# A gated delta rule on ready 32x32 block inverses: seven units of matmuls a step in place of ten, the inverses made in five batches, and the step's loads cut into pieces

## The reference, cut to what matters

```
def gated_delta_chunked(q, k, v, g, beta):          # chunks of 64
    gcum = cumsum(g)                                 # within a chunk
    lower = where(strict, (k*beta) @ k.T * decay, 0)
    sol = triangular_solve(lower + I, [v*beta, k*beta*exp(gcum)])
    u, w = sol
    attn = where(causal, q @ k.T * decay, 0)
    # for each chunk, in order, from state = 0:
    v_new = u - w @ state
    o     = (q*exp(g_i)) @ state + attn @ v_new
    state = state*exp(g_last) + (k*exp(g_last-g_i)).T @ v_new
```

## Time and profile before

| | |
|---|---|
| median of 3 runs | 2506.84 us (2503.91 to 2508.79) |
| the profiled execution | 2497.62 us, its span 2495.9 us |
| TensorE busy | 2326.8 us (93%) |
| VectorE busy | 1422.2 us (57%) |
| ScalarE busy | 1059.5 us (42%) |
| GpSimd busy | 409.1 us (16%) |
| granted TensorE clock, mean | 0.971 |

### The profile page before, as it was taken

How to read it: one execution, slowest core, us unless ns; L and a number is a source line. 1 busy time by engine, 2 the same in 40 slices (tenths; PEclk the granted TensorE clock), 3 DMA queues, 4 the chain that set the end, 5 groups by cost and what they waited for, 6 DMA issues and landing times. The chain is left out here.

```text
span 2495.9 us, 48533 instructions
## 1 busy us (share of the span) xinstructions
PE 2326.8 (93%) x20242; PEld 2071.0 (83%) x20242; DVE 1422.2 (57%) x1792; ACT 1059.5 (42%) x1561; POOL 409.1 (16%) x393
## 2 busy tenths in 40 slices
PE   6999999999999999778878999899999999999996
PEld 5777888999999888677854555599999999999996
DVE  6555311245555286343445458777777777777775
ACT  4666310011111186000035553266666666666664
POOL 1000000012111176433323110000010000100001
PEclk8999999999999999898989999999999999999998
DMA  3333422268676476755544431477778777787765
GB/s 121 89 88 106 141 82 105 72 182 280 203 217 203 154 206 196 231 156 155 155 155 143 149 121 64 178 265 264 255 261 279 272 254 272 263 270 261 267 226 200
DMA packets 174025, 471.69 MB, mean 189 GB/s; under 512 B 57216, under 2 KB 102912, under 8 KB 141088
## 3 DMA queue, kind: packets, MB, share of 16 engines
q1 hardware_dynamic: 160800, 423.08, 50.6%
q0 software_dynamic: 13024, 45.70, 6.4%
HBM read 365.15 MB, written 107.49 MB: 189 GB/s over the span
## 5 line engine op out<-in xcount | busy, mean ns | idle before, releaser
L78 DVE TENSOR_TENSOR ex_w_rest<-weights,ex_w_rounded 128x2048 fp32r<-128x2048 f32 x192 | 439.5, 2290 | 203.9 <-ACT ex_w_rounded L2755 202.0
L2755 ACT CAST ex_w_rounded<-weights 128x2048 fp32r<-128x2048 f32 x192 | 365.8, 1906 | 12.7 <-PEq L48 12.7
L2647 PE MATMUL ex_g_acc<-ex_xt,ex_w_rounded 128*128 128x320 f32 x1024 | 270.4, 347 | 2.1 <-ACT ex_xt L2767 2.1
L2647 PE MATMUL ex_u_acc<-ex_xt,ex_w_rounded 128*128 128x320 f32 x1024 | 271.7, 348 | 0.0
L2648 PE MATMUL ex_g_acc<-ex_xt,ex_w_rest 128*128 128x160 f32 x1024 | 242.1, 236 | 0.0
L2648 PE MATMUL ex_u_acc<-ex_xt,ex_w_rest 128*128 128x160 f32 x1024 | 242.1, 236 | 0.0
L2648 PEld LDWEIGHTS ex_g_acc<-ex_xt,ex_w_rest 128*128 128x128 f32 x1024 | 196.5, 192 | 0.0
L2648 PEld LDWEIGHTS ex_u_acc<-ex_xt,ex_w_rest 128*128 128x128 f32 x1024 | 196.4, 192 | 0.0
L2647 PEld LDWEIGHTS ex_g_acc<-ex_xt,ex_w_rounded 128*128 128x128 f32 x1024 | 193.1, 189 | 2.5 <-issue 2.5
L2647 PEld LDWEIGHTS ex_u_acc<-ex_xt,ex_w_rounded 128*128 128x128 f32 x1024 | 193.1, 189 | 0.2
L85 PE MATMUL ch_wide<-normed,ch_w_rounded 128*128 128x512 f32 x384 | 153.7, 400 | 2.9 <-PEq L48 2.2
(11 more groups left out here) (421 smaller groups left out, 5541.1 us busy)
## 6 DMA issues: line engine op xcount, KB each, us to landing
weights<-in_w_expert SPq DMA_DIRECT2D x192, 1024.0 KB, 5.2
laq<-sc_laq SPq DMA_DIRECT2D x20, 1024.0 KB, 4.1
dl_la<-laq SPq DMA_DIRECT2D x20, 1024.0 KB, 6.0
tk_w<-in_w_tok SPq DMA_DIRECT2D x10, 1344.0 KB, 6.8
ch_w<-in_w_ch SPq DMA_DIRECT2D x24, 512.0 KB, 5.5
sc_rows<-rows SPq DMA_DIRECT2D x40, 256.0 KB, 6.2
sc_qk<-qkv_ch SPq DMA_DIRECT2D x40, 256.0 KB, 5.9
dl_kv<-qkv_tok SPq DMA_DIRECT2D x40, 256.0 KB, 5.9
```

The costliest lines, as they stand in the source:

```text
L78: return dve.tensor_tensor(out, whole, rounded.bitcast(F32), ALU.subtract)
L2647: pe.matmul(bank[:, 0:2 * SLOTS], hi[:, cols], x.rearrange("p a n -> p (a n)"), start=first, stop=False, skip_group_check=True)
L2755: act.copy(w_hi[:, i % SPLIT], held[:, i % HELD]).then_inc(w_rounded, 1)
```

## The change

**Block inverses.** `BLK` goes from 16 to 32. `inversion` goes, and a class `BlockInverse` takes its place. It inverts 128 blocks at once (4 steps x 2 directions x 8 heads x 2 blocks), one to a partition: 31 rounds of a product and a sum, each waiting for the one before. There are five batches. Batches 0 to 3 are GpSimd's work in tokens, cut into four parts that stand behind the scaled keys of steps 4 to 19. Batch 4 is made in attention. Its scratch takes the place of tables that tokens no longer needs by then.

**The layout in memory.** `diag` and `blocks` are held block by block, so that a batch is one row of 4 KB a partition, while one step's blocks are moved in pieces of 32 numbers (128 bytes): 2 stores in tokens, 4 loads in delta.

**Units.** The 16-row correction goes. A step has seven units in `phase_delta`: from_state, from_query, solve, across, to_state, to_output, correction.

**Loads.** SP's program in delta is written out for all steps. It issues twelve DMAs a step for the step three later (4 `blk`, 2 `kv`, 2 `cols`, and `la` in four factors of 256 KB), each behind one of the units. The first two steps' loads now stand in attention behind tiles 7 and 8, the first 3 MB of the merge weights behind tiles 4, 5 and 6, and the other 2 MB in four pieces behind steps 4, 7, 10 and 13. The first merge tile's loads are issued at step 17.

The diff, cut to its core:

```diff
@@ phase_attention @@
                     if t == LOADED_AHEAD:
-                        load_diagonals(sp)
+                        inverse.load(sp, BATCHES - 1)
+                    if t in MIXER_AT:
+                        load_mixer_first(sp, MIXER_AT.index(t))
+                    if t in BEGUN_AT:
+                        begun.start(sp, io, dr, BEGUN_AT.index(t))
                 store(NT - 3)
-                begun.start(sp, io, dr)
                 store(NT - 2)
-                for blocks_stored, count in blocks_out:
-                    sp.wait_ge(blocks_stored, count)
-                begun.blocks(sp, dr)
                 store(NT - 1)
@@ phase_tokens @@
+                def load_blocks_of(m):
+                    for b in range(2):
+                        sp.wait_ge(diag_stored[b], 32 * (BATCH // 2) * (m + 1))
+                    if m:
+                        sp.wait_ge(inverse.out, 64 * m)
+                    inverse.load(sp, m)
...
                     scaled_keys(s)
+                    if s >= BATCH:
+                        m, part = s // BATCH - 1, s % BATCH
+                        if part == 0:
+                            inverse.begin(pool, m)
+                        inverse.rows(pool, m, PART_ROWS[part], PART_ROWS[part + 1])
+                        if part == BATCH - 1:
+                            inverse.finish(pool, m, m)
@@ BlockInverse @@
+BATCH = 4
+PART_ROWS = (0, 8, 15, 22, BLK - 1)
+    def begin(self, engine, n):
+        engine.wait_ge(self.loaded, 32 * (n + 1))
+        engine.tensor_copy(self.u[0:CH], self.x[0:CH].rearrange("p r c -> p c r")).then_inc(self.lowered, 1)
+        ...
+    def rows(self, engine, n, lo, hi):
+        for m in range(lo, hi):
+            below, known = slice(m + 1, BLK), slice(0, m + 1)
+            shape = [P, BLK - 1 - m, m + 1]
+            ...
+            if done:
+                engine.wait_ge(self.rows_done, done)
+            engine.tensor_tensor(t, self.u[:, below, m:m + 1].to_broadcast(shape), self.x[:, m:m + 1, known].to_broadcast(shape), ALU.mult).then_inc(self.terms, 1)
+            engine.wait_ge(self.terms, done + 1)
+            engine.tensor_tensor(self.x[:, below, known], self.x[:, below, known], t, ALU.add).then_inc(self.rows_done, 1)
@@ loads of a step @@
+        for d in range(2):
+            engine.dma_start(blk[CH * d:CH * d + CH, form], dr["blocks"][form, d, s].rearrange("h k r c -> (k r) h c")).then_inc(loaded, 16)
+def load_factor(engine, dr, la, loaded, s, k):
+    engine.dma_start(la[:, k].rearrange("p h c -> p (h c)"), dr["laq"][s][:, k * NH * CH:(k + 1) * NH * CH]).then_inc(loaded, 16)
@@ phase_delta, SP @@
+                for p in range(STEPS):
+                    s = p + AHEAD_STEPS
+                    sp.wait_ge(ks_done, p + 1)
+                    blocks(s)
+                    sp.wait_ge(qt_done, p + 1)
+                    if p >= 1:
+                        sp.wait_ge(at_done, p)
+                    tokens(s, 0)
+                    sp.wait_ge(v_done, p + 1)
+                    tokens(s, 1)
+                    if p + 1 < STEPS:
+                        sp.wait_ge(lx_done, p + 2)
+                    factor(s, LT)
+                    if p >= 1:
+                        store(p - 1)
+                    sp.wait_ge(kd_done, p + 1)
+                    factor(s, KS)
+                    if p in MIXER_STEPS:
+                        load_mixer(sp, MIXER_STEPS.index(p))
+                    sp.wait_ge(at_done, p + 1)
+                    factor(s, QT)
+                    if p + 1 < STEPS:
+                        sp.wait_ge(corrected, p + 2)
+                    factor(s, AT)
@@ phase_delta, TensorE @@
                     from_state(s, b)
-                    second_update(s, b)
-                    if more:
-                        first(s + 1, nb, ni)
+                    from_query(s, b)
                     solve(s, b)
                     if more:
-                        first_update(s + 1, nb)
-                    outputs(s, b)
+                        across(s + 1, nb, ni)
+                    to_state(s, b)
+                    to_output(s, b)
                     if more:
-                        second(s + 1, nb)
+                        correction(s + 1, nb)
```

More of the change, by code:

```diff
@@ L1422 @@
 LOADED_EARLY = 2
-LOADS = 7
+LOADS = 12
 LT, AT, QT, KS = range(4)
@@ L1531, in turn, with store @@
[L1531 to L1539 removed]
+                def store(s):
+                    sp.wait_ge(o_out, s + 1)
+                    for d, chunk in enumerate(places(s, s >= S_STEPS)):
+                        sp.dma_start(dr["o_delta"][d, chunk * CH:chunk * CH + CH, :], ostage[HD * d:HD * d + HD, s % 2].rearrange("p h c -> p (h c)")).then_inc(stored[s % 2], 16)
@@ L1540, in turn @@
                         first_tile.load(sp, io, dr)
-                ring_steps(sp, turn)
-                for s in range(STEPS - RING, STEPS):
-                    store(s, s, True)
+                store(STEPS - 1)
                 for b in range(2):
@@ L1582, in passed, with product @@
                         pe.sem_inc(pe_turns, 1)
-                def single(bank, lhs, moving, done):
+                def product(bank, lhs, moving, done, start=None, stop=True):
+                    grouped = start is None
                     for wave in range(2):
@@ L1635, in second_update @@
                     passed(s)
-                    for wave in range(2):
-                        for h in range(NH):
-                            for d, rows in enumerate(halves):
-                                if (wave + d) % 2 == 0:
-                                    mm = pe.matmul(xbank[rows, h, :], prod[rows, h, :], xt[rows, b, h, :], start=True, stop=True)
-                                else:
-                                    mm = pe.matmul(obank[rows, h, :], la[b][rows, QT, h, :], state[rows, h, :], start=(h == 0), stop=False, skip_group_check=True)
@@ L1652, in outputs, with across, to_state @@
+                def across(s, b, i):
+                    pe.wait_ge(loaded[b], 16 * LOADS * (i + 1))
+                    pe.wait_ge(x_ready, s + 1)
+                    if not early(s, 1):
+                        pe.wait_ge(xt_out, s)
+                    passed(s)
+                    product(ybank, lambda rows, h: la[b][rows, LT, h, :], lambda rows, h: x[rows, b, h, :], lx_done)
+                def to_state(s, b):
                     pe.wait_ge(v_out, s + 1)
                     pe.wait_ge(prepared, s + 1)
+                    if not early(s, 1):
+                        pe.wait_ge(state_out, s)
@@ L1662, in outputs, with to_output @@
-                    mm.then_inc(os_done, 1)
-                def last_step(s):
-                    return isinstance(s, int) and s == STEPS - 1
+                    product(sbank, lambda rows, h: kd[rows, b, h, :], lambda rows, h: vb[rows, h, :], kd_done)
+                def to_output(s, b):
+                    pe.wait_ge(v_out, s + 1)
+                    passed(s)
+                    product(obank, lambda rows, h: la[b][rows, AT, h, :], lambda rows, h: vb[rows, h, :], at_done, start=False)
@@ L1667, in step, with correction @@
+                def correction(s, b):
+                    pe.wait_ge(prod_out, s + 1)
+                    pe.wait_ge(xt_ready, s + 1)
+                    passed(s)
+                    product(ybank, lambda rows, h: prod[rows, h, :], lambda rows, h: xt[rows, b, h, :], corrected)
                 def step(s, b, i, prompt):
-                    more = not last_step(s)
+                    more = not (isinstance(s, int) and s == STEPS - 1)
                     nb, ni = (b + 1) % RING, i + (b + 1) // RING
@@ L1680, in _ @@
                 keep_busy(pe, ubank[:, 0, 0:P], ident, 4)
-                first(0, 0, 0)
+                across(0, 0, 0)
                 keep_busy(pe, ubank[:, 0, 0:P], ident, 2)
-                first_update(0, 0)
+                correction(0, 0)
                 keep_busy(pe, ubank[:, 0, 0:P], ident, 2)
-                second(0, 0)
                 ring_steps(pe, step)
```

371 lines of the change are left out of this document (157 added, 214 removed).

## The result

The changed kernel takes 2463.84 us (median of 4 runs, 2458.96 to 2466.16), the kernel before in the same comparison 2507.06: a ratio of 0.984 (0.982 to 0.986), 43 us faster. That is the forecast direction and half the forecast size; 2464 lies 6 us above the range. A second run of the same kernel gave 0.984 (0.982 to 0.987).

The account below looks back on a forecast made before the run. TensorE, busy 93% of the span, was taken as the bound, so removed matmuls count in full. Delta -81, handover -9 and tokens +5 sum to -85 us: 2417 us, range 2382 to 2458.

Parts of the forecast that it names:

- The handover: Attention to delta: batch 4 ends early, SP no longer waits, delta starts near 996.3 for 1005.5: -9 us.
- I take 9.2 us for a step with loads: Delta: TensorE 8.6, SP 8.0 and DMA engines 8.6 us don't overlap perfectly, so 9.2 us a step.
- fourteen take 8.0 us: Delta, SP's limit: twelve loads and two stores a step at 0.57 us each, 8.0 us.
- the change doesn't do what it says: Delta: a DMA costs SP 1.0 us for 0.57, so 14 us a step; 2494 us, chance 0.05.
- 8.6 us by the forecast: Delta, TensorE's limit a step: 6.7 us for seven units plus 1.9 us of instruction-fetch stalls.
- The 0.95 a unit: Delta: TensorE's price of one unit, from a 9.52 us interval of ten units without loads.
- the first rival: Delta: DMA engines are the bound, 128-byte pieces near 35 ns, step of 11.5 us; 2455 us, chance 0.20.
- 190.8: Delta from start to last state update, in us, against 271.9 before: -81 us.
- Tokens and attention: Ahead of delta: +5 us (0 to 15) charged for VectorE's stretched rows, the thin GpSimd cover and begun loads.
- cycle about 62: Tokens: GpSimd's 57 us a batch plus handing over x, about 8 partly hidden, fits four steps of 63.2 us.
- GpSimd lags a little: Tokens: batches 20% longer make a cycle of 71 us against 63.2; +16 us, 2433 us, chance 0.12.
- the signs named in advance: Wrong if TensorE waits in tokens for factors, delta starts after 1000, or the mean step is outside 8 to 11 us.

Follow-up runs that it names:

- new layout: The changed kernel with block inverses held in memory in delta's reading order, so block loads read rows of 1 KB: 2465.1 us, ratio 0.984.
- the one that only takes DMAs away: The changed kernel with a step's four factors loaded in one DMA of 1 MB, 11 DMAs a step for 14: 2449.01 us, ratio 0.979.
- with SyncE free: The changed kernel with each step's four block loads issued from ScalarE's program in place of SyncE's: 2456.95 us, ratio 0.983.

## Why the prediction was wrong

**The handover held**: -8.7 us for -9, by the mechanism forecast (batch 4 takes 45.0 us for 46 and is done early, the last stores right behind the last unit). Delta still starts at 1023.6, because everything ahead of it is late.

**Delta's step failed: "I take 9.2 us for a step with loads".** It was taken a little above a maximum of three limits, and two of the three were too small.

- SyncE, which sets the step in the changed kernel: "fourteen take 8.0 us" took the price of 0.57 from rows in which a block load is 128 pieces of 512 bytes; it is 512 pieces of 128 bytes now. Measured are 0.77 and 10.8 us. Two edits that take the small pieces away from it (block loads left out; new layout) bring the price to between 0.65 and 0.68; the one that only takes DMAs away has 0.85 and shortens the step all the same. This is the mechanism of the rival "the change doesn't do what it says", at half of its extra price per DMA; it had a chance of 0.05, with the argument that no row had a DMA so slow. No row had a DMA of such pieces at all, so that argument was worth nothing.
- TensorE, 8.6 us by the forecast: with SyncE free it takes 10.3, of which 7.9 us are units (for 6.7) and 2.3 stalls (for 1.9). The 0.95 a unit was read at the full clock and without loads. Over the phase a unit cost 1.04 at a clock of 0.93 before, and 1.12 at 0.89 in that run. There was no term for it, though the forecast's own rows left room for one: 9.52 and 2.7 us of stalls are 12.2, and the interval was 13.06.
- Stalls: in the changed kernel itself TensorE waits 2.6 us a step, as against 2.7 before, but they are other waits. 1.0 are stalls, below the forecast 1.9, and 1.6 are waits for `x` and for the output copy, both behind SyncE. The price per fetch isn't fixed: outside the jumps the stalls are 0.5 us a step without loads and 1.9 with loads and SyncE free.
- DMA engines: the share of 0.75 for a step of 10.8 is 8.1 us, below the forecast 8.6, and a 128-byte piece takes 13.9 ns, not the 17.6 taken or the 35 of the first rival, which falls by that. The rule of the Trainium skill ("DMA: Bandwidth & Descriptors", Specifications) that transfers under 512 bytes don't reach line rate agrees with the same rows: 4.20 MB in such pieces took 14.7%, and 35.76 MB of the other transfers 61.1%, so a byte took twice as long. But the price that set the step stood at the queue that issues them. Its rule on instruction fetch ("Runtime: NRT & Kernel Launch", Instruction fetch mechanics) that a crossing of 16 KB is mostly hidden, and that branches break this, agrees with the run without loads: 0.5 us of stalls in an ordinary step, 4.3 and 4.9 at the two jumps. Beside loads the crossings are not hidden.

Of the 25.5 us by which delta missed its 190.8, the start to the first update gave 3.3 back (10.7 for 14). The last three intervals, taken as free of loads, cost 8.2 (29.8 for 21.6): the last load is issued at 1223.5, past the first of them, and the first merge tile's loads follow; only the last, at 7.4, is as forecast. The sixteen others, jumps included, cost 20.6. The jumps were forecast at +4 each; they were +6 and +7 over the other steps.

**Tokens and attention failed too: +27 for +5.** The step was "cycle about 62". It was 70. The prediction's own terms were 57 and 8, that is 65 against a cover of 63.2, and it counted a part of the 8 as hidden. Measured are 45.1 us of operations for 38.9, since they stretch beside VectorE in tokens (the prediction had the stretching only the other way round), and 6 to 12 us in which a batch waits for its `diag`. A late batch then holds SyncE, SyncE the loads, and so TensorE. That is near to the rival "GpSimd lags a little" in size (a cycle of 71, +16; +14.4 were measured), which had 0.12; it was taken as unlikely, with a cover of 1 us in 63. Not seen at all was the barrier: GpSimd's last stores of the phase are issued at 870.0, behind the last batch (+6.5). And the begun loads, charged in the 5, cost 5.9 alone.

Three of the signs named in advance show it: TensorE waits in tokens (7.2 us, for a load that was issued late), delta starts after 1000, and the scaled keys of step 19 stand 26 us later than before. The mean step stayed inside 8 to 11 us, and SyncE had no gaps.

The cases were taken as alternatives of which one happens; the rival of tokens and a dear step happened together. Moving the work of tokens (18 us), the begun loads (7) and SyncE's DMAs (about 1.4 us a step) brings the time to 2416, close to the forecast 2417; that is a coincidence of size, but it says where the expected gain lay.

## What to carry to other kernels

A queue that issues DMAs is an engine with a busy time of its own: count its DMAs a step, and price small-pieced ones from a row with such pieces, or allow for a good deal more than the usual. Work put beside a phase needs cover against a 15% error, not against none, its price should be read beside the same neighbours, and the wait for its input counts. When units of matmuls are removed, what each costs should be read at the clock of the whole phase. And a gap that the profile calls "issue" should be held against the last rows of every engine that the instruction waits for: an edit that changes nothing in the time may have removed one wait and laid bare another.

## What the runs showed of the hardware

The load right behind four DMAs of 512 pieces each takes the issuing engine 1.6 us in the mean and up to 2.6, where it takes 0.50 to 0.54 when these DMAs are left out, stand on another queue, or read rows of 1 KB. A packet of 128 bytes takes 13.9 ns of a DMA engine. At a jump back of the loop TensorE stalls for 5.2 and 7.0 us beside loads and for 4.3 and 4.9 without; in the other steps it stalls 1.9 us beside loads (with SyncE free) and 0.5 without. GpSimd's operations of 31 to 256 elements a partition take 7.5 us more a batch of 62 in tokens than in attention, all but 0.3 of it in rows that overlap one of VectorE's. Whether the lower clock would go with shorter waits alone was not tried.
